# A pre-norm handed to the matmuls tile by tile: one fused VectorE product, one fused ScalarE round, and the first two weight slots interleaved

## The reference

```python
def modulate(y, i):
    return rms_norm(y, g_pre[i]) * (1.0 + mod[:, i, 1]) + mod[:, i, 0]

x = residual(x, swiglu(modulate(x, 0), f_in[0], f_out[0]), 0, FFN_RES_WEIGHT)
mix, ... = mixer(modulate(x, 1), ...)
x = residual(x, mix, 1, 1.0)
x = residual(x, swiglu(modulate(x, 2), f_in[1], f_out[1]), 2, FFN_RES_WEIGHT)
```

## Time and profile before

| | |
|---|---|
| time, median of 3 runs | 1395.11 us (1386.66, 1395.11 and 1395.72) |
| span of the profiled execution | 1383.3 us |
| TensorE matmuls | 1335.2 us busy, 97% of the span |
| VectorE, ScalarE, GpSimd | 676.9, 553.8 and 85.1 us busy |
| HBM traffic | 249.26 MB read, 4.89 MB written |

### The profile page before, as it was taken

How to read it: one execution, slowest core, us unless ns; L and a number is a source line. 1 busy time by engine, 2 the same in 40 slices (tenths; PEclk the granted TensorE clock), 3 DMA queues, 4 the chain that set the end, 5 groups by cost and what they waited for, 6 DMA issues and landing times.

```text
span 1383.3 us, 23276 instructions
## 1 busy us (share of the span) xinstructions
PE 1335.2 (97%) x10138; PEld 1239.3 (90%) x10138; DVE 676.9 (49%) x695; ACT 553.8 (40%) x661; POOL 85.1 (6%) x103
## 2 busy tenths in 40 slices
PE   5999999999999999999999999999999989999997
PEld 3899999969969699999969999998898769999996
DVE  3434344457875544444354344444677664444433
ACT  4433333353445633333353333334443554333331
POOL 0000000000270000000000000000027100000000
PEclk9999999999999999999999999999999999999999
DMA  9965566374326643446366544646541473444531
GB/s 368 356 240 183 207 212 248 125 267 176 122 95 249 229 148 138 152 162 259 136 252 211 184 140 142 261 159 213 213 142 60 143 275 111 140 148 147 192 143 38
DMA packets 50373, 255.44 MB, mean 185 GB/s; under 512 B 7022, under 2 KB 12014, under 8 KB 30062
## 3 DMA queue, kind: packets, MB, share of 16 engines
q1 hardware_dynamic: 50110, 253.08, 50.3%
q0 software_dynamic: 176, 1.09, 0.2%
HBM read 249.26 MB, written 4.89 MB: 184 GB/s over the span
## 4 chain that ended last, share of the span: by engine, by line
PE 92%; DVE 3%; ACT 2%; issue 1%; DMA 1%; SPq 0%; DVEq 0%; ACTq 0%
PE PS L508 27%; PE PS L510 27%; PE PS L509 27%; PE PS L520 3%; PE PS L558 2%; DMA z<-in_ada 1%; PE PS L688 1%; PE PS L707 1%; ACT sq L1026 1%; PE PS L730 1%; PE PS L908 0%; PE PS L653 0%; DVE raw L1586 0%; PE PS L566 0%; DVE y L1387 0%
## 5 line engine op out<-in xcount | busy, mean ns | idle before, releaser
L508 PE MATMUL PS<-hmh,WHI 128*128 128x320 f32 x1856 | 577.4, 311 | 14.0 <-DVE hml L1327 13.5
L509 PE MATMUL PS<-hml,WHI 128*128 128x320 f32 x1856 | 571.9, 308 | 0.0
L510 PE MATMUL PS<-hmh,WLO 128*128 128x320 f32 x1856 | 571.8, 308 | 0.0
L1274 DVE TENSOR_TENSOR WLO<-raw,WHI 128x2048 fp32r<-128x2048 f32 (+1 forms) x148 | 365.5, 2470 | 397.1 <-ACT WHI L993 397.1
L993 ACT ACTIVATE WHI<-raw 128x2048 fp32r<-128x2048 f32 (+1 forms) x148 | 303.9, 2053 | 352.1 <-PE PS L510 348.9
L508 PEld LDWEIGHTS PS<-hmh,WHI 128*128 128x128 f32 x1856 | 348.7, 188 | 34.7 <-issue 29.3
L509 PEld LDWEIGHTS PS<-hml,WHI 128*128 128x128 f32 x1856 | 348.8, 188 | 0.3
L510 PEld LDWEIGHTS PS<-hmh,WLO 128*128 128x128 f32 x1856 | 348.7, 188 | 0.0
L508 PE MATMUL PS<-hhl,WHI 128*128 128x320 f32 x704 | 216.6, 308 | 0.0
L509 PE MATMUL PS<-hhl,WHI 128*128 128x320 f32 x704 | 216.5, 308 | 0.0
L510 PE MATMUL PS<-hhl,WLO 128*128 128x320 f32 x704 | 216.5, 308 | 0.0
(11 more groups left out here) (239 smaller groups left out, 825.5 us busy)
## 6 DMA issues: line engine op xcount, KB each, us to landing
raw<-in_w_in SPq DMA_DIRECT2D x88, 1024.0 KB, 4.8
raw<-in_w_out SPq DMA_DIRECT2D x32, 1408.0 KB, 5.9
stage<-in_ada_w SPq DMA_DIRECT2D x82, 512.0 KB, 7.6
ada<-in_ada_w SPq DMA_DIRECT2D x46, 512.0 KB, 5.0
raw<-in_m_in SPq DMA_DIRECT2D x20, 1024.0 KB, 4.8
raw<-in_m_out SPq DMA_DIRECT2D x8, 1024.0 KB, 4.9
z<-in_ada SPq DMA_DIRECT2D x3, 1024.0 KB, 12.9
big<-in_ada SPq DMA_DIRECT2D x2, 1024.0 KB, 19.2
```

The costliest lines, as they stand in the source:

```text
L508: mm(out, hi, rhi, start=first, stop=False)
L509: mm(out, hi, rlo, start=False, stop=False)
L510: return mm(out, lo, rhi, start=False, stop=last)
L1274: tt(WLO[:, slot, 0:width], raw[:, slot, 0:width], WHI[:, slot, 0:width].bitcast(F32), ALU.subtract).then_inc(s_lo[slot], 1)
```

## The change

In norms 1 to 5 only:

- VectorE's `prompt` becomes one `scalar_tensor_tensor` for each tile, (x times the tile's scale) times `rst`; 8 in place of 5 groups.
- ScalarE adds the shift and rounds in one activation from `sq` into `hmh`, with bias alone; the in-place pass and the wait on itself are gone. `sq` so holds the value without its shift.
- VectorE's `low_prompt` adds the shift again and subtracts the high part, in one operation for each tile.
- The samples go in two groups of tiles, `TOKS`: tiles 0 and 1, then 2 to 7. Each has its own multiply, shift, rounding copy (ScalarE, behind the prompt tiles 0 and 1) and low part.
- TensorE's `entry` takes tiles of both slots as they come: slot 0 of k = 0 and 1, slot 1 of k = 0, slot 0 of k = 2 and 3, slot 1 of k = 1, and so on; last, slot 1 of k = 4 to 7.
- In the first step after a norm ScalarE rounds the next weights of slot 0 ahead of the evacuation of banks 0 and 1.
- The modulation piece that stood between the two slots in norm 3's first step stands behind both.

```diff
-FEEDS = ((0, 1), (1, 2), (2, 4), (4, 6), (6, 7), (7, 8))
+TOKS = ((0, 2), (2, 8))
...
+            def entry(n, g, second, free):
+
+                def tile(slot, k):
+                    for t in (0, 1):
+                        last = product(slot, t, k)
+                    if k == KT - 1:
+                        last.then_inc(s_used[slot], 1)
+
+                for k in range(KT):
+                    pe.wait_ge(s_hml, KT * n + k + 1)
+                    tile(0, k)
+                    if k == 1:
+                        split_ready(1, g)
+                        pe.wait_ge(second, free)
+                    if k % 2:
+                        tile(1, k // 2)
+                for k in range(KT // 2, KT):
+                    tile(1, k)
...
-                    pair(0, 0, norm)
+                    if norm is not None:
+                        entry(norm, g, s_uread, (2 * l + f) * IT_IN + it + 1)
+                        for p in pieces:
+                            partial(p)
+                        return
+                    pair(0)
...
-                    pair(0, 0, 3 * l + 1 if it == 0 else None)
+                    if it == 0:
+                        entry(3 * l + 1, g, s_zd, 5 * l + 1)
+                        continue
+                    pair(0)
...
-                for i, (a, b) in enumerate(FEEDS):
-                    act.wait_ge(s_mt, fed(n) + i + 1)
-                    feed(fed(n) + i, m, a, b, KT + n)
+                for k in range(KT):
+                    act.wait_ge(s_mt, KT * n + k + 1)
+                    a_(hmh[:, k, 0:TP], sq[:, k, 0:TP], ACT.Identity,
+                       bias=mod[m][:, 8 + k, 0:1]).then_inc(s_hmh, 1)
+                    if k < len(TOKS):
+                        a, b = TOKS[k]
+                        act.wait_ge(s_ms, KT + 2 * (n - 1) + k + 1)
+                        a_(hmh[:, a:b, TP:T], sq[:, a:b, TP:T], ACT.Copy).then_inc(s_hs, 1)
...
+                    if it == 0:
+                        hi_split(0, g + 1, width)
                     act.wait_ge(s_used[0], g + 2)
                     act.wait_ge(s_uread, i + 1)
                     a_(sg, PS[:, 0:2, 0:T], ACT.Silu).then_inc(s_gread, 1)
-                    hi_split(0, g + 1, width)
+                    if it:
+                        hi_split(0, g + 1, width)
...
-            def prompt(a, b):
-
-                tt(sq[:, a:b, 0:TP], x[:, a:b, 0:TP], rst[:, 0:TP].unsqueeze(1).to_broadcast([P, b - a, TP]),
-                   ALU.mult).then_inc(s_mt, 1)
+            def prompt(m, k):
+
+                stt(sq[:, k, 0:TP], x[:, k, 0:TP], mod[m][:, 16 + k, 0:1], rst[:, 0:TP],
+                    ALU.mult, ALU.mult).then_inc(s_mt, 1)
+
+            def low_prompt(n, m, k):
+
+                dve.wait_ge(s_hmh, KT * n + k + 1)
+                stt(hml[:, k, 0:TP], sq[:, k, 0:TP], mod[m][:, 8 + k, 0:1], hmh[:, k, 0:TP].bitcast(F32),
+                    ALU.add, ALU.subtract).then_inc(s_hml, 1)
...
-                scaled = ch.mark(tt(ys.rearrange("p k (b t) -> p k b t", t=TS), seq(x), by_seq(mod[m], 16, KT), ALU.mult))
+                ch.link(tt(ys.rearrange("p k (b t) -> p k b t", t=TS), seq(x), by_seq(mod[m], 16, KT), ALU.mult))
...
+                done = rooted(0)
+                prompt(m, 0)
+                added(0, done)
+                prompt(m, 1)
+                low_samples(n, 0)
+                low_prompt(n, m, 0)
+                done = rooted(1)
+                low_prompt(n, m, 1)
+                added(1, done)
+                prompt(m, 2)
+                prompt(m, 3)
+                low_samples(n, 1)
+                for k in range(2, KT):
+                    low_prompt(n, m, k)
+                    if k + 2 < KT:
+                        prompt(m, k + 2)
```

More of the change, by code:

```diff
@@ L255, in chunk_of @@
             return 3 * n + j
-        def fed(n):
-            return KT + len(FEEDS) * (n - 1)
         def home(p):
@@ L304, in trunk @@
         s_hml = sem("s_hml")
+        s_hs = sem("s_hs")
         s_ms = sem("s_ms")
@@ L318, in trunk @@
         ev = {}
-        for n in ("e f g b d0 e0 z0 ends eb kh0 kh itp it ktp kt gr am ds dss obk oev osq ost orr og oh "
-                  "lv us un vm dsm s0n rot qk vtp vt sc scd ex exn pt ptd pv pvd ss ssd sex sexn spt sptd spv spvd "
-                  "cv cst mixl kvo exd at lbd lbe gs sc0 ob sn rp ssd2 sd ebq dec dsr rcs rch sr").split():
+        for n in ("f g b d0 e0 z0 ends eb kh0 kh itp it ktp kt gr am ds dss obk oev osq ost orr og oh "
+                  "lv us un vm dsm s0n rot qk vtp vt scd ex exn pt ptd pv pvd ssd sex sexn cv cst mixl "
+                  "kvo exd lbd lbe gs sc0 ob sn rp sd ebq dec dsr rcs rch sr").split():
             ev[n] = sem("e_" + n)
@@ L533, in split_ready, with product, pair @@
                 pe.wait_ge(s_lo[slot], g + 2)
[L535 to L541, removed]
-                    for k in range(KT):
[L543 to L546, removed]
-                    for t in (0, 1):
[L548 to L552, removed]
+            def product(slot, t, k):
+                return mm3(PS[:, 2 * slot + t, 0:T], slot, k * 256 + t * P, hmh[:, k, :], hml[:, k, :],
+                           k == 0, k == KT - 1)
+            def pair(slot, half=False):
+                for t in (0, 1):
+                    for k in range(KT):
+                        last = product(slot, t, k)
+                    if half and t == 0:
+                        last.then_inc(s_half, 1)
+                last.then_inc(s_used[slot], 1)
+            def entry(n, g, second, free):
+                def tile(slot, k):
+                    for t in (0, 1):
+                        last = product(slot, t, k)
+                    if k == KT - 1:
+                        last.then_inc(s_used[slot], 1)
+                for k in range(KT):
[8 more added lines that the diff above has]
+                    tile(1, k)
             def x_stats(n):
@@ L581, in body @@
                     pe.wait_ge(s_uread, (2 * l + f) * IT_IN + it + 1)
-                    pair(1, 2)
+                    pair(1)
                 if n == 0:
@@ L972, in _ @@
                         pe.wait_ge(s_sqp, 12 * l + 6)
-                        pair(0, 0)
+                        pair(0)
                     split_ready(1, g)
@@ L976, in _ @@
                         pe.wait_ge(s_sqp, 12 * l + 7)
-                    pair(1, 2, half=it == 1)
+                    pair(1, half=it == 1)
                 gap(3 * l + 1, AT_OUT[l])
@@ L1223, in _ @@
                         silu_set()
+                    if it == 0:
+                        hi_split(0, g + 1, W_IN)
                     act.wait_ge(s_used[0], g + 2)
@@ L1227, in _ @@
                        scale=-1.0 if 4 * it == Z_F else 1.0).then_inc(s_za, 1)
-                    hi_split(0, g + 1, W_IN)
+                    if it:
+                        hi_split(0, g + 1, W_IN)
                     if it == 0:
@@ L1307, in normed, with low_samples @@
                    ALU.mult).then_inc(s_mt, 1)
-            def prompt(a, b):
-                tt(sq[:, a:b, 0:TP], x[:, a:b, 0:TP], rst[:, 0:TP].unsqueeze(1).to_broadcast([P, b - a, TP]),
-                   ALU.mult).then_inc(s_mt, 1)
+            def prompt(m, k):
[5 more added lines that the diff above has]
+                    ALU.add, ALU.subtract).then_inc(s_hml, 1)
+            def low_samples(n, i):
+                a, b = TOKS[i]
+                dve.wait_ge(s_hs, 2 * (n - 1) + i + 1)
+                tt(hml[:, a:b, TP:T], sq[:, a:b, TP:T], hmh[:, a:b, TP:T].bitcast(F32), ALU.subtract)
             def samples(a, b):
@@ L1340, in x_norm, with rooted, added @@
                 dve.wait_ge(s_x, KT * (n + 1))
-                scaled = ch.mark(tt(ys.rearrange("p k (b t) -> p k b t", t=TS), seq(x), by_seq(mod[m], 16, KT), ALU.mult))
+                ch.link(tt(ys.rearrange("p k (b t) -> p k b t", t=TS), seq(x), by_seq(mod[m], 16, KT), ALU.mult))
                 dve.wait_ge(s_r, n + 1)
[L1343 to L1354, removed]
+                def rooted(i):
+                    a, b = TOKS[i]
+                    return ch.mark(tt(ys[:, a:b], ys[:, a:b], rst[:, TP:T].unsqueeze(1).to_broadcast([P, b - a, NB * TS]),
+                                      ALU.mult))
+                def added(i, done):
+                    a, b = TOKS[i]
+                    ch.wait(done)
+                    tt(seq(sq)[:, a:b], ys[:, a:b].rearrange("p k (b t) -> p k b t", t=TS), by_seq(mod[m], 8 + a, b - a),
+                       ALU.add).then_inc(s_ms, 1)
+                done = rooted(0)
[14 more added lines that the diff above has]
+                        prompt(m, k + 2)
             def first_norm():
```

## The result

| | before | after |
|---|---|---|
| time, median | 1386.74 us (8 runs, 1382.96 to 1395.72) | 1375.87 us (8 runs, 1373.48 to 1380.68) |
| ratio, 95% interval | | 0.9922 [0.9905, 0.9939] |
| profiled execution: span | 1383.3 us | 1374.1 us |
| mean granted clock over it | 0.990 | 0.992 |

The change made the kernel 10.9 us faster, 0.8%, against a forecast of 1.4 us. The median of before, with five runs more, lies 8.4 us under the one that the forecast was added to.

A forecast was written before the change was run, and what follows sets the result against it. TensorE, busy 1335.2 us or 97% of the span, was taken to bound the kernel. Savings and stalls at the five norm entries summed to -1.39 us, from the median of 1395.11 to 1393.7; range 1384.3 to 1399.4.

The forecast's parts named there:

- The chain: Norm entries, inverse root to first low part: TensorE starts 2.38 us after VectorE's first operation, not 3.32; 0.94 us sooner.
- Rival A: Second step of norms 1, 2, 4, 5: new stall paid, waits stay; +4.3 us, 1399.4; chance 0.20.
- the waits that the prediction adds up: TensorE's idle times before first products and tile 2 in norms 1 to 5: seven rows and norm 1's two, 13.3 us.
- errata section: VectorE in the norms: fixed latency per instruction, so splitting should lose; 1.25 us of added VectorE time per norm.
- Only 24 of slot 1 remain: Second step of every entry: 3.52 us of cover for a 4.73 us weight split, a 1.06 us stall; norm 3 0.07.
- Tile 2's wait: TensorE's wait for tile 2's low part in norms 1, 3 and 4: 0.37 us in place of 1.01, saving 0.64.
- Norm 5's low stretch: After norm 5's gap: 12 products at 1.2 GHz, 0.26 us each, kept as before; norm 5 in all +0.24 us.
- Rival C: Norm 5's shorter gap, 3.81 for 4.63, leaves the clock at 2.4 GHz: -1.0 us more, 1392.7; chance 0.15.
- Norms 1 and 4: Their entries: -1.58 us from earlier first products and tile 2, +1.06 for the weight split's stall; -0.52 each.
- Norm 2: Its entry: only its 0.25 us wait can be lost, against the stall of 1.06; +0.81 us.
- Norm 3: Its entry: -0.83 first product, -0.64 tile 2, +0.07 stall left behind the modulation piece; -1.40 us.
- Rival B: All entries: TensorE starts once free, the split hides, all 13.5 us of waits go; -14.9 us, 1380.2; chance 0.03.

The follow-up runs named there:

- six fill products: The changed kernel with 6 products that nobody needs on TensorE in the gap ahead of norm 5; 1377.21 us, ratio to before 0.9913.
- entry-only run: The kernel before with the interleaved entry and the rounding ahead of the evacuation, its old norm kept; 1382.82 us, ratio 0.9976.

## Why the prediction was wrong

**The chain was right.** Fused operations took 0.48 us as taken, bias alone 0.51 where scale and bias had taken 0.60, and the first product came at 2.35 against 2.38. Rival A, which needed over 0.54 us or a chain of 3.32, falls. (Of the waits that the prediction adds up, has six and not seven; the 13.3 us are right.) By the errata section of the Trainium skill's "VectorE: DVE Perf Modes", which advises large tiles, the splitting should lose. VectorE did pay for it, 7.1 us in all (6.3 forecast). But its sum is not on the path, and the latency to the first low part is; with the samples in one tile of 512 the run was 5.2 us slower at equal clock. The trace agrees with the advice for VectorE's own time; on the way to the first product the measurement goes against it.

**"Only 24 of slot 1 remain": the step that failed.** The order puts a tile of slot 1 behind every odd k, and k = 7 is odd, so tile 3 of slot 1 stands behind slot 0's last product. I took slot 0's last for the 72nd of 96; it is the 66th. (The text ahead of the prediction has the same slip: `s_used0` rises after the 11th of 16 groups of products, not the 12th.) Thirty products remain, 4.40 us (313.62 to 318.02), and the split needs 318.36 - 313.62 = 4.74, as the sum of rows had it (4.73). The stall is 0.19 and not 1.06, in four entries 3.5 us. The run with 24 products of cover returned 1.08 and shows this.

**Tile 2's wait was mis-sized**, -1.00 in place of -0.64, three times. A listed idle time starts at the listed end of a pipelined product, 0.16 us after the next one could have begun, so what I took off for 1.01 was 1.17. And the low part that ended at 306.56 was used at 306.61: handing over to TensorE took 0.05 there, while I had put in the 0.15 of the first product. The trace of before had shown it. Its low part of tile 2 ends at 306.67, and TensorE starts at 306.72:

```profile
305.84 0.83 DVE L1327 TENSOR_TENSOR hml<-sq,hmh 128x640 fp32r<-128x640 f32 x1 [0.73 <-ACT hmh L1031]
```

The last 0.10 is in the chain: the low part came 0.04 sooner after VectorE's start than I had added up, and TensorE asked 0.06 later. Each time 0.36, together 1.1 us.

**Norm 5's low stretch is not fixed.** I had kept it at 12 products. In the profile compared here it was 20; eight more at 0.26 for 0.147 us cost 0.9, about what the shorter wait had brought (4.63 to 3.80). In the second profile of the same kernel it was about 13, so the 0.9 belongs to the execution and is not shown to come from the change. Rival C, the clock staying up, is refuted by both profiles; the six fill products show that the stretch can be avoided.

**The sum redone.** Norms 1 and 4: -0.52 - 0.87 - 0.36 = -1.75 (measured -1.66, -1.65). Norm 2: +0.81 - 0.87 = -0.06; its row is tile 2 and not the first product, and by the starts (468.65 and 469.20) it had cost 0.40 and not 0.25, so -0.15 more; and a piece that landed with 1.48 us of waiting where it was 2.27, -0.79, makes -1.00 (-0.94). That transfer is not shown to have to do with the change: in the second profile of the changed kernel the wait was 0.9 us. Norm 3: -1.40 - 0.07 - 0.36 = -1.83 (-1.85). Norm 5: +0.24 - 0.87 + 0.9 = +0.27 (+0.11). In all -6.1 against -5.99. The fit leaves out the 0.9 of norm 5's clock, so 6.9 of the counted stretches stand beside its 7.7 (standard error 0.5).

**The rest of the miss is the baseline and the clock.** The forecast added a difference to a median of three runs, of which two were at 1395; eight give 1386.74. Of the 17.8 us by which 1393.7 missed, 8.4 are this, and 9.5 the effect: 4.6 in the stretches of the change, which the two steps above make up (what norm 2 gave, norm 5 took), and 4.9 outside them. Of these some 3 to 4 are clock that differs between executions, by the 10.9 of the medians and the 6.7 to 8.0 at equal clock; the rest is open. With the right count alone the forecast would have been 3.5 us lower, 1390.2, and still too high. The doubt was named (the spread of 9.1 us), but the range was drawn around the high median, with its lower end 2.4 below the lowest run. Rival B's time, 1380.2, was nearer than the forecast's, its mechanism was not there: 6.6 us of waits remain and the low clock stayed.

## What to carry to other kernels

When an edit reorders two streams, count the cover in the listed order, to the last instruction: one tile of six products decided here whether a stall of 1.06 us was paid in four entries. Where TensorE waits for a short chain, add up that chain's latency and not an engine's busy time; small first groups can pay although they cost the engine more. Take off for a wait the whole gap between starts, less the spacing. And do not put down a stretch of low clock in one profile to the change before a second profile of the same kernel shows it too.

## What the runs showed of the hardware that I had not expected

- One kernel on one chip (before, 35 runs) ran at mean granted clocks of 0.983 to 0.995. At 1.02 us for each 0.001 that is 12 us, more than any edit here moved at equal clock. Stretches at 1.2 GHz came at other places in other profiles. In the entry-only run norm 3's gap of 2.21 us was followed by one, and before, the same gap of 2.20 was not. The stretch from 720 in the entry-only run, and then before (clock after the busy times):

```profile
720.00:725.00 5.00, 5.00 (x28) 5.00 (x28) 3.13 (x6) 4.58 (x9) 0.00 (x0) 0.76 0.02 3
```

```profile
720.00:725.00 5.00, 5.00 (x38) 4.81 (x41) 2.06 (x4) 3.52 (x6) 0.00 (x0) 1.00 0.01 3
```

- The gap ahead of norm 5 does not settle how long the clock is low behind it. The changed kernel, with 3.80 and 3.79 us of gap, had 5.25 us at 1.2 GHz in one profile and about 3.5 in the other, begun only after eight products; before, with 4.63, had 3.13. Why, no run here tells.
- A product of unrounded float32, 128 x 320, has two records and took 0.55 us where one of rounded operands takes 0.147.
- VectorE to TensorE took 0.14 to 0.15 us at the first product of an entry and 0.05 to 0.07 at tile 2, wherever TensorE waited for them. How long TensorE had been idle does not tell them apart: in before tile 2's 0.05 came after 1.01 us listed idle, and in the changed kernel the first product's 0.14 after 0.72. Why, no run here tells.
